# Hybrid diffusion trunk on one core: order of the first DeltaNet head's work and of the first loads

## The chip, the cores and the metric

The kernel runs on one core of a Trainium2 chip. The metric is the device time in microseconds (us) of one execution; of several executions the median. Before the change it is 2210.88 us (median of 3 runs, 2209.02 to 2216.32). A profiled execution of its own gives the trace.

TensorE (PE) does the matrix products, VectorE (DVE) and ScalarE (ACT) the elementwise work, GpSimd (POOL) a part of it, SyncE (SP) issues nearly all loads.

## The reference

A trunk of four layers works on 128 context tokens and 256 latent tokens, 1024 features wide. Layers 0 and 3 mix tokens with a gated DeltaNet, layer 1 with grouped-query attention, layer 2 with latent attention. After each mixer comes a mixture of 16 experts. Shift, scale and gate of every sub-layer come from the conditioning vectors ("ada", the modulation).

```
for l in range(DEPTH):
    m = split(silu(cond) @ w_ada[l] + b_ada[l], 6)
    h = x * (1 + m[1]) + m[0]
    o = mixer(h)                                     # gdn, gqa, mla, gdn
    x = layer_norm(ALPHA * x + (1 + m[2]) * o)
    f = moe(x * (1 + m[4]) + m[3])
    x = layer_norm(ALPHA * x + (1 + m[5]) * f)

def gdn(h):                                          # 8 heads, 128 wide
    q, k, v = silu(short_conv(h @ w_qkv))            # 5 taps
    z, a, b = h @ w_z, h @ w_a, h @ w_b
    g, beta = -exp(a_log) * softplus(a + dt_bias), sigmoid(b)
    # per chunk of 64 tokens, both directions: a unit triangular system,
    # then a scan over the chunks with a 128 x 128 state
    o = delta_rule(l2norm(q), l2norm(k), v, g, beta)
    return (rms_norm(o) * silu(z)) @ w_out
```

All is float32. The mixture takes the best group of experts and the two best in it, for each token.

## The kernel before

Tokens are columns: an activation is [128 partitions, 8 blocks of features, 384 tokens], in the tiles `bufx`, `bufh` and `bufo`. Each engine has its own instruction list, written out by hand, and engines meet through semaphores. The order in a list is the order of the code; no scheduler moves anything.

**Loads.** Weights go through `ring`, eight slots of 1 MB (2048 columns), in the fixed order of their use. SP issues a load when the slot's earlier unit has been used (`ring_free`), and counts up `ring_full` of the slot when it lands. At the start SP issues the parameters `par` (1434 columns: conditioning and its bias, 208 columns, come first; then norm gains, taps, router and the weights `w_ab` of a and b), the first two modulation units, the constants `con` (3076 columns: identity, masks, fold matrices), four more units, the input `bufx`, and two more units. Then come the first head's units. All of them use one queue.

**Start.** TensorE multiplies the eight modulation units (L742). DVE turns the rows and adds the bias (L2195, L2197). ACT and DVE modulate x into `bufh` (L1687, L2214). Then TensorE's `gdn` begins: the a/b rows (L851, reads `w_ab`), two steps of the first head's projection (L834), a fold of the a/b rows with a constant matrix (L857), the rest of the projection, and the chunk sums (L865). Before the fold ACT copies the rows to `lnt` (L1675).

**Heads.** A head's work on TensorE has four projections m = 0 to 3 (k, q, v, z), eight contraction steps each (`head_proj`, L834; a step shows as two passes in the trace), row sums (`decay_rows`, L906), Gram products (`gram`, L935), turned keys and values (`k_tokens` L945, `v_tokens` L956), an inversion by small 32 x 32 products (`invert`, L974 and others) and a scan over chunks (`scan`). The projections of head n = h + 1 are cut into pieces and put between the steps of head h's `invert` and `scan`, so that TensorE has work while ACT and DVE take a product. Projection m of head 0 goes to PSUM bank 5 if m is odd, everything else to bank 6. Raw results m = 0 to 2 are copied by ACT (semaphore `raw_in`, three per head), z by `head_z` on ACT (L1731, semaphore `z_in`, one per head). In the scan, `qe` (L1116) starts to write bank 5.

In `invert` of head h, TensorE waits for DVE's turned tile (`inv_x`, L2420), does product 1 (L974), then the first two steps of head h + 1's projection, its first row sums and the value tokens:

```
pe.wait_ge(inv_x, hh * X_STEPS + X_AT["ndt"])
product(hh, 1)
if more:
    head_proj(l, n, 0, 0, 2)
    decay_rows(l, n, 0)
v_tokens(l, h)
```

The value tokens wait for DVE's decayed keys (`kd_done`, L2398) and the third silu on ACT.

**Layer norms.** After the root, DVE multiplies eight tiles (L2245, `normed`, one each). ACT modulates tiles 0 to 4 of the next `bufh` (L1680), DVE tiles 5 to 7 (L2252, two instructions a tile). GpSimd's `scale_residual` writes ALPHA times the normalised x to `bufx` (L2935, eight instructions), for the next residual. It waits first for all of `bufh` (`wait_all_h`). In layer 3 GpSimd's `gdn` follows with three memsets of scratch (L2959 to L2961; ACT waits for them by `pad_zero`). In the mixtures TensorE multiplies the router (L1545), and a chain of small DVE instructions (L2667 to L2696) picks the experts, before TensorE goes on with L1570.

Of the kernel before, what the change touches and what calls it, by code (L numbers as in the profile page):

```python
# [360 lines left out]
def trunk(nc, I, O):  # L361

    unit_at, n_units = unit_plan()
    with ExitStack() as ctx:
# [152 lines left out]

        params_in, consts_in, x_in = sems("params_in consts_in x_in")
        ring_full = [sem(f"ring_full{i}") for i in range(RING)]
# [138 lines left out]
        def _(sp):  # L658
            sp.dma_start(par[:, :], I["params"]).then_inc(params_in, 16)

# [9 lines left out]
            for n, pair in enumerate(START_PAIRS):  # L670
                for x in range(2):
                    load(I["w_ada"][2 * pair + x], 2 * n + x)
                if n == 0:
                    sp.dma_start(con[:, :], I["consts"]).then_inc(consts_in, 16)
                if n == 2:
                    sp.dma_start(bufx[:, :, :], I["x"]).then_inc(x_in, 16)
            for l, kind in enumerate(KINDS):
                u0, uo = unit_at["mix", l], unit_at["out", l]
                if kind == "gdn":
                    order = gdn_order(l)  # L680
                    for n, (what, h, k) in enumerate(order):
                        if what == "w":
                            load(I["gdn_w_in"][li_of[l] * 2 * H + 2 * h + k], u0 + n)
                        else:
                            load(I["w_ada"][2 * ADA_AT["head", l] + 4 * h + k], u0 + n)
# [43 lines left out]
        def _(pe):  # L729
# [90 lines left out]
            def head_proj(l, n, m, k0=0, k1=KT):  # L820
# [3 lines left out]
                if k0 == 0:  # L824
                    landed(pe, u)
                    if m == 0:
                        pe.wait_ge(z_in, nn)
                    elif n:
                        pe.wait_ge(raw_in, nn * 3 + m)
                    elif m >= 2:  # L830
                        pe.wait_ge(raw_in, nn * 3 + m - 1)
# [13 lines left out]
            def gdn(l):  # L845
# [7 lines left out]
                last.then_inc(ab_mm, 1)  # L853
                head_proj(l, 0, 0, 0, 2)
                pe.wait_ge(ab_act, 2 * li + 1)
                for t in range(TT):
# [149 lines left out]
            def invert(l, h):  # L1006
# [4 lines left out]
                if h:  # L1011
                    pe.wait_ge(s_done, hh * 10)
                pe.wait_ge(inv_x, hh * X_STEPS + X_AT["ndt"])
                product(hh, 1)
                if more:
                    head_proj(l, n, 0, 0, 2)
                    decay_rows(l, n, 0)
# [72 lines left out]
            def scan(l, h):  # L1090
# [21 lines left out]
                def qe(r):  # L1112

                    for d in range(2):
                        s = SCAN[r, d]
# [540 lines left out]
            for n in range(4):  # L1656
                for x in range(2):
                    ada_unit(n, 2 * n + x, x, START_BANKS[n % 2])
            pe.wait_ge(consts_in, 16)
            for l, kind in enumerate(KINDS):  # L1660
# [9 lines left out]
        def _(act):  # L1670
# [502 lines left out]
            first_modulated(0, 4)  # L2173
            act.wait_ge(consts_in, 16)
            act.wait_ge(mod_ready, 4)
            first_modulated(4, H_ACT)
            for l, kind in enumerate(KINDS):
                {"gdn": gdn, "gqa": gqa, "mla": mla}[kind](l)
# [6 lines left out]
        def _(dve):  # L2185
# [717 lines left out]
            for n in range(4):  # L2903
                ada_add(START_PAIRS[n], 2 * n + 1, n, START_BANKS[n % 2])
            dve.wait_ge(consts_in, 16)
            for l, kind in enumerate(KINDS):
                if l == 0:
                    dve.wait_ge(x_in, 16)
                    dve.wait_ge(mod_ready, 4)
                    first_modulated()  # L2910
                else:
                    dve.wait_ge(mod_ready, (l + 1) * (ADA_UNITS // 2))
# [7 lines left out]
        def _(pool):  # L2920
# [3 lines left out]
            def scale_residual(n):  # L2924

                if n == 0:
# [4 lines left out]
                    return  # L2931
                wait_all_h(pool, n)
                for k in range(KT):
# [116 lines left out]

            pool.wait_ge(params_in, 16)
            for part, name in enumerate(("ln_g", "ln_b")):
# [93 lines left out]
```

## Time and profile before

| | us |
|---|---|
| median of 3 runs | 2210.88 |
| the profiled execution, its own time | 2213.71 |
| its span, first to last instruction | 2211.9 |
| PE busy | 2038.2 |
| DVE busy | 1339.1 |
| ACT busy | 1034.5 |
| POOL busy | 244.0 |

In the first of 40 slices of the span the queue moved 378 GB/s. Times in all views are from the start of the span, so they compare with 2211.9; what lies around the span is 1.8 us.

### The profile page before, as it was taken

The page shows a single profiled execution, that of the slowest core. Times are in us where ns is not written, and L with a number is a line of the kernel's source. Part 1 is how long each engine was busy: PE and PEld are TensorE (multiplying, and loading weights), DVE is VectorE, ACT ScalarE, POOL GpSimd, SP SyncE. Part 2 cuts the span into 40 slices and gives each one's busy share as a digit, 9 for nine tenths or more (in the row PEclk, how much of TensorE's full clock was granted, in tenths as well). Part 3 has the DMA queues.
Part 4 walks back from the last instruction along what each step waited for, and adds up shares of the span by engine and source line. Part 5 has one row for each costly group of instructions (what it writes and reads, how often), then busy time and mean ns, then how long its engine had stood idle before and what let it go on. Part 6 is the DMA issues. An engine that isn't in the chain of part 4 may idle for free.

```text
span 2211.9 us, 44967 instructions
## 1 busy us (share of the span) xinstructions
PE 2038.2 (92%) x18880; PEld 1420.3 (64%) x18881; DVE 1339.1 (61%) x2625; ACT 1034.5 (47%) x1783; POOL 244.0 (11%) x363
## 2 busy tenths in 40 slices
PE   6999999898998999899899998998899999988996
PEld 3566666557775665677666665776466666647774
DVE  2566655437896341689722325898656666437896
ACT  3344444226774341576523315765444454226773
POOL 0432222110001000100010001000322232100000
PEclk9999999998999999899999998999999999889998
DMA  9234343345895444488643443887311121025880
GB/s 378 95 131 173 121 151 148 142 153 186 284 318 203 164 173 163 145 310 297 236 151 142 152 172 131 309 303 267 117 45 64 45 69 64 26 79 181 281 299 29
DMA packets 56768, 381.22 MB, mean 172 GB/s; under 512 B 6384, under 2 KB 10480, under 8 KB 12000
## 3 DMA queue, kind: packets, MB, share of 16 engines
q1 hardware_dynamic: 51552, 373.00, 47.2%
q10 hardware_dynamic: 4608, 4.20, 0.5%
q8 instruction: 159, 2.61, 0.5%
q0 software_dynamic: 384, 0.89, 0.1%
q14 instruction: 65, 0.53, 0.1%
HBM read 373.96 MB, written 4.10 MB: 171 GB/s over the span
## 4 chain that ended last, share of the span: by engine, by line
PE 77%; DVE 13%; ACT 5%; issue 3%; DMA 1%; SPq 0%; ACTq 0%; DVEq 0%
PE ps L834 15%; PE ps L1495 6%; PE ps L1499 5%; PE ps L1498 5%; DVE e_wlo L2806 5%; PE ps L786 4%; PE ps L762 4%; PE ps L742 3%; PE ps L974 3%; PE ps L1282 3%; DVE bufx L2824 2%; PE ps L797 2%; ACT e_whi L1675 2%; PE ps L1451 2%; PE ps L1383 2%
## 5 line engine op out<-in xcount | busy, mean ns | idle before, releaser
L2806 DVE TENSOR_TENSOR e_wlo<-ring,e_whi 128x1024 fp32r<-128x1024 f32 x384 | 456.0, 1220 | 94.6 <-ACT e_whi L1675 79.2
L1675 ACT ACTIVATE e_whi<-ring 128x1024 fp32r<-128x1024 f32 x384 | 402.9, 1060 | 120.4 <-PE ps L1499 117.2
L834 PE MATMUL ps<-bufh,ring 128*128 128x384 f32 x1024 | 394.7, 507 | 6.9 <-ACT bufo L1731 4.7
L834 PEld LDWEIGHTS ps<-bufh,ring 128*128 128x128 f32 x1024 | 177.3, 192 | 98.3 <-issue 23.3
L1495 PE MATMUL ps<-e_whi,e_hs 128*128 128x512 f32 x512 | 210.7, 412 | 28.3 <-DVE e_wlo L2806 24.8
L1675 ACT ACTIVATE scratch<-ps 128x384 f32<-128x384 f32 (+6 forms) x311 | 109.1, 368 | 220.5 <-PE ps L834 52.4
L1499 PE MATMUL ps<-e_whi,e_hs 128*128 128x512 f32 x512 | 200.8, 392 | 0.0
L1498 PE MATMUL ps<-e_wlo,e_hs 128*128 128x512 f32 x512 | 199.9, 390 | 0.0
L2935 POOL TENSOR_SCALAR bufx<-bufo,x_gb 128x384 f32<-128x384 f32 x56 | 36.2, 661 | 1104.3 <-DVE bufh L2252 1104.3
L1495 PEld LDWEIGHTS ps<-e_whi,e_hs 128*128 128x128 f32 x512 | 96.0, 188 | 69.2 <-ACT e_whi L1675 41.8
L2338 DVE SCALAR_TENSOR_TENSOR scratch<-scratch,par 128x386 f32<-128x386 f32 x192 | 128.4, 669 | 4.8
L742 PE MATMUL ps<-ring,silc 128*32 128x128 f32 x3072 | 105.8, 292 | 20.1 <-DMA ring<-in_w_ada 20.1
L1675 ACT ACTIVATE scratch<-ps,scratch 128x128 f32<-128x128 f32 x96 | 31.8, 365 | 194.6 <-PE ps L1129 192.9
L1495 PE MATMUL ps<-e_whi,e_hidT 128*128 128x512 f32 x256 | 103.2, 403 | 13.3 <-issue 9.2
L1499 PEld LDWEIGHTS ps<-e_whi,e_hs 128*128 128x128 f32 x512 | 96.0, 188 | 21.9
L742 PEld LDWEIGHTS ps<-ring,silc 128*32 128x32 f32 x3072 | 87.8, 117 | 33.8 <-DMA ring<-in_w_ada 15.6
L1498 PEld LDWEIGHTS ps<-e_wlo,e_hs 128*128 128x128 f32 x512 | 96.4, 188 | 16.6
L1675 ACT ACTIVATE lnt<-ps 128x384 f32<-128x384 f32 x26 | 12.7, 490 | 195.5 <-PE ps L797 178.6
L1498 PE MATMUL ps<-e_wlo,e_hidT 128*128 128x512 f32 x256 | 102.2, 399 | 0.0
L1499 PE MATMUL ps<-e_whi,e_hidT 128*128 128x512 f32 x256 | 101.7, 397 | 0.0
L974 PEld LDWEIGHTS ps<-scratch 32*32 32x32 f32 x6144 | 64.8, 107 | 54.7 <-issue 37.2
L2224 DVE SCALAR_TENSOR_TENSOR bufh<-ps,mod,bufx 128x128 f32<-128x128 f32 x64 | 23.4, 412 | 118.9 <-PE ps L762 77.3
(312 smaller groups left out, 3525.1 us busy)
## 6 DMA issues: line engine op xcount, KB each, us to landing
ring<-in_moe SPq DMA_DIRECT2D x192, 1024.0 KB, 4.9
ring<-in_w_ada SPq DMA_DIRECT2D x96, 1024.0 KB, 6.8
ring<-in_gdn_w_in SPq DMA_DIRECT2D x32, 1024.0 KB, 6.6
ring<-in_gdn_w_out SPq DMA_DIRECT2D x8, 1024.0 KB, 4.8
ring<-in_gqa_w_in SPq DMA_DIRECT2D x6, 1024.0 KB, 4.8
ring<-in_gqa_w_out SPq DMA_DIRECT2D x4, 1024.0 KB, 6.7
ring<-in_mla_w_out SPq DMA_DIRECT2D x4, 1024.0 KB, 7.8
ring<-in_mla_w_in SPq DMA_DIRECT2D x3, 1024.0 KB, 4.9
```

The source lines that it names most:

```text
L742: last = mm(ps[32 * g:32 * g + 32, bank, 0:P], silc[:, kt, :], w[:, k, g, :], start=(kt == 0), stop=(kt == KT - 1))
L762: last = mm(ps[:, banks[t % len(banks)], 0:T], w[:, t % 2, kt, :], rhs[:, kt, :], start=(kt == 0), stop=(kt == KT - 1))
L786: last = mm(ps[:, banks[t % len(banks)], 0:T], w[:, t % 2, kt, :], bufo[:, kt, :], start=(kt == 0), stop=(kt == KT - 1))
L834: last = mm(ps[:, head_bank(n, m), 0:T], w[:, m % 2, kt, :], bufh[:, kt, :], start=(kt == 0), stop=(kt == KT - 1))
L974: last = mm(ps[quarter(g), bank, at:at + 32], g_inv[a][quarter(g), d, t, :], g_inv[b][quarter(g), d, t, :], start=True, stop=True)
L1282: last = mm(ps[:, bank, 0:T], w[:, pos % 2, kt, :], bufh[:, kt, :], start=(kt == 0), stop=(kt == KT - 1))
L1495: first = mm(out, parts[0], whi, start=start, stop=False)
L1498: mm(out, parts[0], wlo, start=False, stop=False)
L1499: return mm(out, parts[1], whi, start=False, stop=stop)
L1675: return op(out, in_, ACT.Copy, **kw)
L2338: done = stt(acc, g_cin[:, m, tap:tap + CONVW], taps[:, tap:tap + 1], acc, ALU.mult, ALU.add)
L2806: return tt_(e_wlo[:, b, :], w, e_whi[:, b, :].bitcast(F32), ALU.subtract)
```

## The change

- SP loads the parameters in two parts: the first 208 columns at the start (`params_in`), the other 1226 behind the eighth modulation unit (`rest_in`). x goes behind the fourth unit, consts behind the first head's first unit.
- The waits for consts move behind the first modulation on ACT and DVE, and behind the a/b rows on TensorE. GpSimd waits for the second part of the parameters before its first instruction.
- In `invert` of head 0, in both DeltaNet layers, the two steps of head 1's projection stand ahead of the wait for the turned tile. They wait for head 0's three raw copies, and not for its z copy. The scan's `qe` waits for z in head 0.
- GpSimd's `scale_residual` no longer waits for all of `bufh`, except for the first one.

```diff
-            sp.dma_start(par[:, :], I["params"]).then_inc(params_in, 16)
+            first_params = PARAMS["ln_g"][0]
+            sp.dma_start(par[:, 0:first_params], I["params"][:, 0:first_params]).then_inc(params_in, 16)
...
-                if n == 0:
-                    sp.dma_start(con[:, :], I["consts"]).then_inc(consts_in, 16)
-                if n == 2:
+                if n == 1:
                     sp.dma_start(bufx[:, :, :], I["x"]).then_inc(x_in, 16)
+            sp.dma_start(par[:, first_params:PARAM_COLS], I["params"][:, first_params:PARAM_COLS]).then_inc(rest_in, 16)
...
                             load(I["gdn_w_in"][li_of[l] * 2 * H + 2 * h + k], u0 + n)
+                            if l == 0 and n == 0:
+                                sp.dma_start(con[:, :], I["consts"]).then_inc(consts_in, 16)
... TensorE, head_proj
-                    if m == 0:
+                    if m == 0 and n == 1:
+                        pe.wait_ge(raw_in, nn * 3)
+                    elif m == 0:
                         pe.wait_ge(z_in, nn)
... TensorE, gdn
                 head_proj(l, 0, 0, 0, 2)
+                pe.wait_ge(consts_in, 16)
                 pe.wait_ge(ab_act, 2 * li + 1)
... TensorE, invert
+                if h == 0:
+                    head_proj(l, n, 0, 0, 2)
                 pe.wait_ge(inv_x, hh * X_STEPS + X_AT["ndt"])
                 product(hh, 1)
                 if more:
-                    head_proj(l, n, 0, 0, 2)
+                    if h:
+                        head_proj(l, n, 0, 0, 2)
                     decay_rows(l, n, 0)
... TensorE, scan, qe
+                    if r == 0 and h == 0:
+                        pe.wait_ge(z_in, hh + 1)
... TensorE, before the layers
-            pe.wait_ge(consts_in, 16)
+            pe.wait_ge(rest_in, 16)
... ACT
             first_modulated(0, 4)
-            act.wait_ge(consts_in, 16)
             act.wait_ge(mod_ready, 4)
             first_modulated(4, H_ACT)
+            act.wait_ge(rest_in, 16)
+            act.wait_ge(consts_in, 16)
... DVE
-            dve.wait_ge(consts_in, 16)
...
                     first_modulated()
+                    dve.wait_ge(rest_in, 16)
+                    dve.wait_ge(consts_in, 16)
... GpSimd, scale_residual, n > 0
-                wait_all_h(pool, n)
... GpSimd, before the layers
-            pool.wait_ge(params_in, 16)
+            pool.wait_ge(rest_in, 16)
```

On SP, the loads of the start before the change (the last number is columns):

```order
L659 DMA par<-in_params 128x1434
L664 DMA ring<-in_w_ada 128x2048 x2
L674 DMA con<-in_consts 128x3076
L664 DMA ring<-in_w_ada 128x2048 x4
L676 DMA bufx<-in_x 128x3072
L664 DMA ring<-in_w_ada 128x2048 x2
L664 DMA ring<-in_gdn_w_in 128x2048 x3
```

and after it:

```order
L660 DMA par<-in_params 128x208
L665 DMA ring<-in_w_ada 128x2048 x4
L675 DMA bufx<-in_x 128x3072
L665 DMA ring<-in_w_ada 128x2048 x4
L676 DMA par<-in_params 128x1226
L665 DMA ring<-in_gdn_w_in 128x2048
L685 DMA con<-in_consts 128x3076
L665 DMA ring<-in_gdn_w_in 128x2048 x2
```

The constants, and most of the parameters, moved from ahead of the last modulation units to behind them.

On TensorE, the end of head 0's projections and the start of its inversion, before the change (L945 turned keys, L974 small products, L906 row sums, L956 value tokens):

```order
L945 MATMUL ps<-con,scratch 128x128 x2
L834 MATMUL ps<-bufh,ring 128x384 x2
L974 MATMUL ps<-scratch 32x32 [waits inv_x]
L974 MATMUL ps<-scratch 32x32 x23
L834 MATMUL ps<-bufh,ring 128x384 [waits z_in,ring_full2]
L834 MATMUL ps<-bufh,ring 128x384
L906 MATMUL ps<-con,scratch 128x128 [waits s_done]
L906 MATMUL ps<-con,scratch 128x128 x2
L956 MATMUL ps<-con,scratch 64x128 [waits silu_done,kd_done]
```

and after it, under its own line numbers (L950 keys, L838 projection, L979 small products, L911 row sums, L961 value tokens):

```order
L950 MATMUL ps<-con,scratch 128x128 x2
L838 MATMUL ps<-bufh,ring 128x384 x2
L838 MATMUL ps<-bufh,ring 128x384 [waits raw_in,ring_full2]
L838 MATMUL ps<-bufh,ring 128x384
L979 MATMUL ps<-scratch 32x32 [waits inv_x]
L979 MATMUL ps<-scratch 32x32 x23
L911 MATMUL ps<-con,scratch 128x128 [waits s_done]
L911 MATMUL ps<-con,scratch 128x128 x2
L961 MATMUL ps<-con,scratch 64x128 [waits silu_done,kd_done]
```

The two projection steps moved from behind the first small product to ahead of it, and wait for `raw_in` where they waited for `z_in`.

## Rows read from the trace of the kernel before

**Rows 1.** Chain of waits, 0 to 75 us: start us, us, what

```profile
5.91 27.66 DMA ring<-in_w_ada
...
40.66 3.97 PE ps L834 x12
```

**Rows 2.** Timeline, 30 to 40 us: start us, us, engine line op out<-in xcount [idle before]

```profile
31.13 1.94 PE L742 MATMUL ps<-ring,silc 128*32 128x128 f32 x32 [4.24 <-DMA ring<-in_w_ada]
...
38.62 0.49 ACT L1675 ACTIVATE lnt<-ps 128x384 f32<-128x384 f32 x1 [1.81 <-PE ps L851]
```

**Rows 3.** Timeline, layer 0, 64 to 77 us, head 0's inversion

```profile
64.36 1.46 PE L834 MATMUL ps<-bufh,ring 128*128 128x384 f32 x4
...
66.70 9.72 POOL L2929 TENSOR_SCALAR bufx<-bufx 128x384 f32<-128x384 f32 x8
...
67.49 0.62 PE L974 MATMUL ps<-scratch 32*32 32x32 f32 x48 [1.68 <-DVE scratch L2420]
...
69.40 1.02 DVE L2398 TENSOR_TENSOR scratch<-ps,scratch 128x384 f32<-128x384 f32 x2
...
70.54 2.90 PE L834 MATMUL ps<-bufh,ring 128*128 128x384 f32 x4 [2.43 <-ACT bufo L1731]
...
75.87 1.05 PE L974 MATMUL ps<-scratch 32*32 32x32 f32 x96
```

**Rows 4.** Timeline, layer 3, 1600 to 1606 us, head 0's inversion

```profile
1600.19 1.02 DVE L2398 TENSOR_TENSOR scratch<-ps,scratch 128x384 f32<-128x384 f32 x2
...
1605.12 0.88 PE L956 MATMUL ps<-con,scratch 128*64 128x128 f32 x12
...
1605.92 1.05 PE L974 MATMUL ps<-scratch 32*32 32x32 f32 x96
```

**Rows 5.** Stretches: length, busy of each engine (instructions), granted clock, DMA share, GB/s

```profile
core 0: us, PE busy (x) PEld busy (x) DVE busy (x) ACT busy (x) POOL busy (x), PEclk, DMA share, GB/s
70.00:74.00 4.00, 3.46 (x8) 2.28 (x9) 0.80 (x2) 0.62 (x3) 4.00 (x4) 0.50 0.01 2
495.30:497.86 2.56, 0.40 (x4) 0.16 (x2) 2.41 (x7) 1.20 (x3) 2.56 (x5) 1.00 0.04 13
1575.00:1580.00 5.00, 5.00 (x16) 3.79 (x17) 3.49 (x8) 3.16 (x7) 0.00 (x0) 0.50 0.00 0
```

**Rows 6.** Timeline, layer 3, 1565 to 1592 us, entry of the DeltaNet

```profile
1565.06 5.16 POOL L2935 TENSOR_SCALAR bufx<-bufo,x_gb 128x384 f32<-128x384 f32 x8 [212.34 <-DVE bufh L2252]
...
1567.10 0.75 PE L857 MATMUL ps<-con,lnt 128*128 128x32 f32 x6
...
1570.20 3.06 DVE L2275 TENSOR_SCALAR scratch<-scratch 128x48 f32<-128x48 f32 x1
...
1573.58 1.55 PE L865 MATMUL ps<-scratch,con 128*128 128x24 f32 x8 [1.78 <-DVE scratch L2279]
...
1591.58 0.88 PE L935 MATMUL ps<-scratch 128*64 128x128 f32 x12
```

**Rows 7.** Timeline, layer 0, 39 to 61 us, the same three operations

```profile
39.91 0.75 PE L857 MATMUL ps<-con,lnt 128*128 128x32 f32 x6
...
44.45 0.97 PE L865 MATMUL ps<-scratch,con 128*128 128x24 f32 x8
...
60.54 0.88 PE L935 MATMUL ps<-scratch 128*64 128x128 f32 x12
```

**Rows 8.** Timeline, layer 0, 489 to 499 us, layer norm and router

```profile
489.72 1.01 DVE L2245 TENSOR_TENSOR bufo<-bufh,ps 128x384 f32<-128x384 f32 x2
...
490.65 1.82 DVE L2252 TENSOR_SCALAR bufh<-bufo,h_gb 128x128 f32<-128x128 f32 x6
...
495.83 0.17 DVE L2674 TENSOR_TENSOR lnt<-lnt 128x24 f32<-128x24 f32 x1
...
498.96 0.39 PE L1570 MATMUL ps<-e_rs,con 128*128 128x12 f32 x1 [3.26 <-DVE e_rs L2696]
```

**Rows 9.** Timeline of DVE, L2335 with GpSimd idle and with it busy

```profile
45.24 0.42 DVE L2335 TENSOR_SCALAR scratch<-scratch,par 128x386 f32<-128x386 f32 x1 [1.35 <-ACT scratch L1675]
...
65.47 0.81 DVE L2335 TENSOR_SCALAR scratch<-scratch,par 128x386 f32<-128x386 f32 x1
```

More of the change, by code:

```diff
@@ L515, in trunk @@
         e_cnt = sb("e_cnt", [P, NG])
-        params_in, consts_in, x_in = sems("params_in consts_in x_in")
+        params_in, rest_in, consts_in, x_in = sems("params_in rest_in consts_in x_in")
         ring_full = [sem(f"ring_full{i}") for i in range(RING)]
```

## The prediction, on record before the changed kernel ran

> **What bounds the kernel now.** I read the chain of waits of the first 75 us, then the timeline of the same stretch, then the same places in layer 3, then the layer norms. The start is bound by the loads: the chain goes from 5.91 us through one DMA of 27.66 us, the last of the eight modulation units; it lands at 5.91 + 27.66 = 33.57, and from there the projections of TensorE (L834) are in the chain [rows 1]. The reader is to see that nothing on an engine sets the first 33 us, only bytes on one queue: units arrive 33.57 - 31.13 = 2.45 us apart [rows 1, 2]. After that TensorE is almost always busy, and what can be won are its holes. Two alike are around the first head of each DeltaNet layer. In layer 0 TensorE ends a projection at 64.36 + 1.46 = 65.82, waits 1.68 us for DVE, does one product (0.62), waits 2.43 us for the z copy on ACT, and then runs four passes of the next projection in 2.90 us where the same four took 1.46 just before, because the granted clock is 0.50, its lower level of 1.2 GHz [rows 3, 5]. Layer 3 has the same picture [rows 4].
>
> **The head's projection.** The first two contraction steps of head 1's projection (four passes of L834) go ahead of the wait for the turned tile, and wait for the three raw copies only. Their bank was last read by the third raw copy, long done at 65.8; their weights came before the holes. So they fill 65.8 to 67.3 and the product still starts at 67.49. What is late next: six passes of row sums (L906), done near 69.0, then the value tokens (L956), which wait for DVE's L2398, ending at 69.40 + 1.02 = 70.42 [rows 3]. Twelve passes of L956 take 0.88 at the full clock [rows 4]. The two products of L974 that started at 75.87 then start at 70.42 + 0.06 + 0.88 = 71.36: 4.5 us earlier. In layer 3: 1600.19 + 1.02 + 0.06 + 0.88 = 1602.15 instead of 1605.92, 3.8 us earlier [rows 4]. What follows is the same cadence of products and ACT and DVE steps, moved as a whole. The new wait for z in front of the scan's first L1116 costs nothing: z is copied just before 70.54, the products at 75.87 come after that, and the scan after the products [rows 3]; behind the wait stand only passes of the same head. What hides the row sums, the wait for L2398, leaves 1.5 us of TensorE idle; see the clock below.
>
> **The loads.** By the last modulation unit 3076 columns of consts and 1226 of 1434 columns of parameters are no longer ahead. At 2.45 us for 2048 columns that is 3.68 + 1.47 = 5.15 us: it lands at 28.42. The rest of the parameters lands at 29.89, the head's first unit at 32.34, the consts at 36.02. TensorE needs the parameters at about 29.8 for L851 and the head unit at 33.5, so neither costs more than 0.1. But ACT now takes the consts before its copy of the a/b rows. That copy started at 38.62, 5.05 after the last unit [rows 1, 2]; by the unit alone it would start at 33.47, by the consts at 36.07. So the fold (L857) starts at 36.07 + 0.49 (the copy) + about 0.36 (hand-over and weights, an estimate) = 36.92 instead of 39.91 [rows 2, 7]: 3.0 us, not 5.15. Bounds: 0, if the queue gives the consts no earlier than that they are needed now, and 5.15. I take 3.0. GpSimd starts its pads only when the rest of the parameters is there, at 30, and its three memsets took the length of the 3.06 us row at 1570.20 [rows 6]; they end near 34, before ACT first writes into them (about 39). The queue carries the same bytes in all, so the head's second unit lands as before, at 36.02 + 2.45 = 38.5; TensorE comes to it only after passes that end at 40.66 + 3.97 = 44.6 [rows 1].
>
> **The wait taken from GpSimd's residual scaling.** Eight instructions (L2935, 5.16 us in one run) now start behind the first normalised tile and not behind the last modulated one, in seven layer norms. It gives back in two places. First the entry of layer 3. Now the run ends at 1570.2, the memsets follow, and DVE's L2275, 48 columns, takes 3.06 us beside them [rows 6]; TensorE idles 1.78 and the clock is 0.50 from 1575 to 1580 [rows 5, 6]. From the fold to the chunk sums (L857 to L865) layer 0 needs 44.45 - 39.91 = 4.54, layer 3 1573.58 - 1567.10 = 6.48; from there to the Gram products (L935) layer 0 needs 16.09 and layer 3 18.00 [rows 6, 7]. The excess is 1.94 + 1.91 = 3.85, all of which goes if run and memsets are past. Second, the router of every mixture: seven DVE instructions took 2.41 us beside the run where one free of it takes 0.17 [rows 5, 8]. 2.41 - 7 x 0.17 = 1.2, with their overlap about 1.3, and TensorE waits 3.26 us for them [rows 8].
>
> It takes in a third place. The run now lies beside DVE's normalising (L2245) and its six modulating instructions (L2252, 1.82 us), whose end TensorE waits for at once in the router and in layer 3 [rows 8]. L2245 has one input in SBUF; L2398, of the same kind and size, took 1.02 for two with GpSimd busy beside it [rows 3], and two of L2245 with it idle take 1.01 [rows 8]: no cost. L2252 is a tensor_scalar; that kind (L2335) took 0.42 alone and 0.81 beside GpSimd [rows 9], 0.39 more. With three pairs, each waiting once, that is 3 x 0.39 = 1.2, less the slack of the sixth; I take 1.0 per norm. Bounds: 0, and 2.0, if L2252 waits until the whole run is over (it starts 0.55 after L2245 and lasts 5.16; L2252 starts 3.73 after it). In the attention layers the first projection is long enough to hide it. So a mixture gains 1.3 - 1.0 = 0.3, four give 1.2 (bounds -2.8 and 5.2), and layer 3 gains 3.85 - 1.0 - 0.3 = 2.5, the 0.3 for the memsets that now lie beside the first DVE step of the a/b rows (bounds 1.5 and 3.85).
>
> The Trainium skill (SBUF — State Buffer, Practical consequences) says that a DVE instruction with at most one SBUF input and outside the two-port modes does not contend with GpSimd, and that tensor_scalar in such a mode does, the second to issue waiting for the whole of the other's instruction. The trace agrees on both kinds, by the 1.02 against 1.01 and the 0.81 against 0.42 above. It speaks against this part of the change; by it each of the three GpSimd instructions left in the run would hold L2252 for its full length, and the sum would be the first rival's.
>
> **The sum.** 3.0 (start) + 4.5 + 3.8 (heads) + 2.5 (layer 3) + 1.2 (mixtures) = 15.0. From it goes an allowance for the clock. At three places TensorE idles 1.5 to 1.7 us: before the fold at the start, and before the value tokens in both heads. It fell to 1.2 GHz after a hole of 1.78 and after 1.68 and 2.43 with a product between [rows 3, 5, 6]; four passes then cost 2.90 - 1.46 = 1.4 more. One chance in two at each of three places: 2.1. Net 12.9. The profiled execution took 2213.71 (2211.88 span), so it would be 2200.8; the median of the runs before is 2210.88, 2.8 lower, so I forecast 2198.
>
> **Rivals.**
> First, DVE waits out the run in every norm that counts: 2.0 instead of 1.0 at five places, 5 us less, 2203. For it: L2275 was held for all three memsets [rows 6]. Against: in the router DVE got in between instructions of the run, seven within 2.41 us [rows 5]. Chance 0.15.
>
> Second, the heads give nothing: what follows head 0 is paced by the steps of ACT and DVE, or by a clock that falls in the new hole, and the products don't start earlier. 8.3 less in the sum, 2206. For it: an idle of 1.5 remains. Against: none of L2398 and ACT's copies waits for the moved passes. Chance 0.12.
>
> Third, the mixtures gain more: a router hole of 3.26 that becomes 2 or less keeps the clock up for the gathers behind it, some 2 us each, 8 more: 2190. Against: a second hole follows in each router, which may drop it all the same. Chance 0.12.
>
> Fourth, on the other side: the normalising L2245 itself waits for GpSimd. Paced by the run's 5.16 / 8 = 0.65, each of 8 instructions in 7 norms would take up to 0.65 more, 36 us in all: 2198 + 36 = 2234. It decides from 12.9 / 56 = 0.23 us per instruction. Against it stands the 1.02 of L2398. Chance 0.04.
>
> The forecast keeps 0.57. A difference under 0.3%, 6.6 us, can't be told from none. Forecast and third rival are faster, the first rival (7.9 gained) mostly, the second (4.9) is mostly the same: faster 0.80, same 0.14, slower 0.06. The range goes from the third rival with some of its gain left out, 2188, to the second with the upper bounds of DVE's wait, 2207.
>
> **What would show it.** The last modulation unit lands near 28.4, and ACT's first copy waits for the consts, at 36. In both DeltaNet layers the four passes lie ahead of the first product, there is no wait for the z copy, and the passes take 1.5, not 2.9. In layer 3 L2275 takes 0.2 and TensorE has no hole before L865. L2935 starts under L2245; L2252 takes 2.2 to 3.8 in place of 1.82; the seven router instructions take 1.2. Wrong would be a last unit that still lands after 31, L2245 above 0.6 each, or a clock that falls at places where it did not.

## The result and the profile after

| | before | after |
|---|---|---|
| median, us (runs) | 2210.1 (4, 2209.02 to 2216.32) | 2187.2 (4, 2182.55 to 2189.56) |
| the profiled execution, us | 2213.71 | 2186.74 |
| its span, us | 2211.9 | 2184.9 |
| its mean granted clock | 0.966 | 0.973 |

The ratio is 0.9888, with a 95% interval of 0.9863 to 0.9913. By the medians the kernel became 22.9 us faster, where 12.9 was forecast (2198, range 2188 to 2207). The direction was right and the size was wrong: 2187.2 lies just below the range.

I went through the trace of after in the order of the prediction's terms, each time with the same TensorE instruction in both traces: how much earlier does it start now? Lines of the kernel have moved: L834 is L838 now, L857 L862, L865 L870, L906 L911, L935 L940, L956 L961, L974 L979, L1545 L1555, L1570 L1580, L2245 L2256, L2252 L2263, L2275 L2286, L2398 L2409, L2935 L2946.

**The start.** First the timeline of after, 26 to 38 us, of TensorE, DVE and ACT in turn (start us, us, engine line op out<-in xcount [idle before]).

```profile
28.82 1.08 PE L744 MATMUL ps<-ring,silc 128*32 128x128 f32 x32 [0.82 <-DMA ring<-in_w_ada]
30.36 0.85 PE L855 MATMUL ps<-bufh,par 128*32 128x384 f32 x8 [0.46 <-DMA par<-in_params]
...
37.45 0.82 PE L862 MATMUL ps<-con,lnt 128*128 128x32 f32 x6 [1.21 <-ACT lnt L1685]
```

```profile
30.59 3.27 DVE L2225 TENSOR_SCALAR bufh<-bufx,mod 128x128 f32<-128x128 f32 x6
```

```profile
36.82 0.49 ACT L1685 ACTIVATE lnt<-ps 128x384 f32<-128x384 f32 x1 [5.32 <-DMA con<-in_consts]
```

The last modulation unit came near 28.8, and the fold waits for the consts, as forecast. They landed some 0.7 us later than I had worked out (ACT's copy, released by them, starts at 36.82), and the fold starts at 37.45 instead of 39.91 [rows 2, 7]: 2.5 us earlier for a forecast 3.0.

**The head of layer 0.** The timeline of TensorE in after, 61 to 72 us, answers to [rows 3].

```profile
61.98 2.75 PE L838 MATMUL ps<-bufh,ring 128*128 128x384 f32 x8
65.10 0.62 PE L979 MATMUL ps<-scratch 32*32 32x32 f32 x48 [0.38 <-DVE scratch L2431]
65.65 0.93 PE L911 MATMUL ps<-con,scratch 128*128 128x128 f32 x6
68.09 0.88 PE L961 MATMUL ps<-con,scratch 128*64 128x128 f32 x12 [1.50 <-DVE scratch L2409]
68.90 1.05 PE L979 MATMUL ps<-scratch 32*32 32x32 f32 x96
69.87 1.56 PE L838 MATMUL ps<-bufh,ring 128*128 128x384 f32 x4
```

The picture is the forecast one: the wait of 1.68 is 0.38, the wait of 2.43 for the z copy is gone, and one of 1.50 for L2409 is left. The four moved passes are the last of the eight in the first row, which take 2.75 together: about 1.4 for four, and not 2.90. (The four of 69.87 are the next two steps, which were there before.) The product pair starts at 68.90 instead of 75.87. Of these 6.97 us 2.4 came from the start, so the head gave 4.6, forecast 4.5.

**The entry and the head of layer 3.** The timeline of TensorE in after, 1551 to 1592 us.

```profile
1553.81 0.75 PE L862 MATMUL ps<-con,lnt 128*128 128x32 f32 x6
...
1558.35 0.97 PE L870 MATMUL ps<-scratch,con 128*128 128x24 f32 x8
...
1574.42 0.88 PE L940 MATMUL ps<-scratch 128*64 128x128 f32 x12
...
1584.24 1.54 PE L961 MATMUL ps<-con,scratch 128*64 128x128 f32 x12 [1.38 <-DVE scratch L2409]
1585.71 1.50 PE L979 MATMUL ps<-scratch 32*32 32x32 f32 x96
```

Two rows of DVE, from its timeline of 1544 to 1560 us, are its modulating instructions and the one that had been held:

```profile
1548.89 2.70 DVE L2263 TENSOR_SCALAR bufh<-bufo,h_gb 128x128 f32<-128x128 f32 x6
...
1556.56 0.19 DVE L2286 TENSOR_SCALAR scratch<-scratch 128x48 f32<-128x48 f32 x1
```

The hole of 1.78 before the chunk sums is gone, and DVE's L2286 takes 0.19 where L2275 had taken 3.06. Fold to chunk sums is 1558.35 - 1553.81 = 4.54, the same as in layer 0; on to the Gram products it is 16.07. So 1.94 + 1.93 = 3.9 came in, as worked out, and 0.9 was paid ahead of it, where L2263 takes 2.70 and L2252 took 1.82. In this head the clock did fall in the hole that the edit leaves: twelve passes of L961 take 1.54, not 0.88. The pair of products starts at 1585.71 instead of 1605.92, 20.2 earlier, and 17.2 of it was there at the Gram products: 3.0 for the head, forecast 3.8.

**The mixtures.** The timeline of DVE and then of TensorE in after, in the norm and the router of layer 0, answers to [rows 8].

```profile
486.15 2.71 DVE L2263 TENSOR_SCALAR bufh<-bufo,h_gb 128x128 f32<-128x128 f32 x6
...
491.69 0.18 DVE L2684 TENSOR_TENSOR lnt<-lnt 128x24 f32<-128x24 f32 x1
```

```profile
493.83 0.39 PE L1580 MATMUL ps<-e_rs,con 128*128 128x12 f32 x2 [1.73 <-DVE e_rs L2707]
```

L2263 takes 2.71 where L2252 took 1.82: the 0.9 that it pays for running beside GpSimd, forecast 1.0. The router's wait is 1.73 instead of 3.26: 1.5 gained, forecast 1.3. The difference, 0.6, is what the instructions themselves give; 0.3 was forecast. But a mixture gave more than that. From the norm to 20 us behind the router the four gained 2.0, 3.4, 2.0 and 1.2 us in this trace. (Counted from the first L2245 of the norm to the first product with an expert's weights, some 21 us behind the rank products L1570; 0.5 to 0.6 of each gain is there when the rank products start, the rest comes behind them.) Three stretches show where, as busy time of the engines and the granted clock: 32 us from the norm of mixtures 0 and 1, and 22 us at the end of layer 3's mixer, first before, then after.

```profile
487.00:519.00 32.00, 23.71 (x173) 19.23 (x166) 21.93 (x70) 16.01 (x29) 5.76 (x11) 0.71 0.18 69
893.00:925.00 32.00, 23.91 (x173) 18.67 (x166) 22.00 (x70) 16.20 (x31) 5.75 (x11) 0.73 0.19 69
...
1918.00:1940.00 22.00, 20.03 (x116) 14.78 (x116) 5.50 (x19) 2.58 (x7) 1.56 (x4) 0.61 0.02 7
```

```profile
481.00:513.00 32.00, 25.20 (x182) 19.66 (x182) 21.42 (x71) 17.55 (x31) 6.07 (x11) 0.73 0.23 82
884.00:916.00 32.00, 24.83 (x187) 19.28 (x186) 22.27 (x71) 18.39 (x34) 6.06 (x11) 0.79 0.20 69
...
1900.00:1922.00 22.00, 19.81 (x136) 13.52 (x135) 9.22 (x24) 3.14 (x9) 1.56 (x4) 1.00 0.02 7
```

The columns are those of [rows 5]; the one to read is the granted clock, the third from the end: 0.71 and 0.73 before, 0.73 and 0.79 after. Behind the routers TensorE runs for less time at 1.2 GHz. At the end of layer 3's mixer the clock is 1.00 instead of 0.61, worth 6 us in this pair, at a place which the change doesn't touch.

So the terms at the instructions held, and what is left to explain, some 10 us, looks like clock. Theory A: the routers' shorter hole keeps the clock up, and GpSimd's part of the change gives far more than its instructions do. Theory B: work is moved as a whole, and the clock falls elsewhere by luck, whichever part moves it.

### The profile page after: what moved, and what is told of

Same layout as the page of the kernel before. It is cut to its first block, busy times and chain, and to the rows that moved or that the text cites. A ratio compares the mean times of both kernels' runs of the same rounds, so it can differ in the third digit from the quotient of the medians.

```text
span 2184.9 us, 44966 instructions
## 1 busy us (share of the span) xinstructions
PE 2021.1 (92%) x18880; PEld 1403.4 (64%) x18881; DVE 1338.0 (61%) x2625; ACT 1034.3 (47%) x1783; POOL 246.5 (11%) x363
## 4 chain that ended last, share of the span: by engine, by line
PE 76%; DVE 13%; ACT 5%; issue 4%; DMA 2%; ACTq 0%; SPq 0%; DVEq 0%
PE ps L838 15%; PE ps L1505 6%; DVE e_wlo L2817 5%; PE ps L1509 5%; PE ps L1508 5%; PE ps L788 4%; PE ps L764 4%; PE ps L744 3%; PE ps L979 3%; PE ps L1292 3%; DVE bufx L2835 2%; PE ps L799 2%; PE ps L1461 2%; ACT e_whi L1685 2%; PE ps L1393 2%
## 5 line engine op out<-in xcount | busy, mean ns | idle before, releaser
L838 PE MATMUL ps<-bufh,ring 128*128 128x384 f32 x1024 | 392.4, 505 | 2.0 <-ACT scratch L1685 0.7
L838 PEld LDWEIGHTS ps<-bufh,ring 128*128 128x128 f32 x1024 | 177.0, 191 | 93.9 <-issue 18.3
L1505 PE MATMUL ps<-e_whi,e_hs 128*128 128x512 f32 x512 | 210.5, 411 | 28.2 <-DVE e_wlo L2817 24.8
L2946 POOL TENSOR_SCALAR bufx<-bufo,x_gb 128x384 f32<-128x384 f32 x56 | 37.6, 685 | 1072.5 <-DVE bufo L2256 1072.5
L979 PEld LDWEIGHTS ps<-scratch 32*32 32x32 f32 x6144 | 65.5, 108 | 55.9 <-issue 40.5
```

What stands on the lines that cost most here:

```text
L838: last = mm(ps[:, head_bank(n, m), 0:T], w[:, m % 2, kt, :], bufh[:, kt, :], start=(kt == 0), stop=(kt == KT - 1))
L979: last = mm(ps[quarter(g), bank, at:at + 32], g_inv[a][quarter(g), d, t, :], g_inv[b][quarter(g), d, t, :], start=True, stop=True)
L1505: first = mm(out, parts[0], whi, start=start, stop=False)
```

## Experiments

Twelve experiments, in three groups of four; each group shared one chip and its own runs of the kernel before. Gains below are (1 - ratio) times the median of before in that group (2208.75, 2211.12 and 2210.5 us), with the interval's ends. They can be up to 3.5 us off the plain difference of the medians. By this formula the first comparison above is 24.8 (19.2 to 30.3).

### The three parts alone, and the whole once more

`only_head` has the edits in `head_proj`, `invert` and `scan`, `only_loads` those of the loads and the waits for them, and `only_pool` is this line alone:

```diff
             def scale_residual(n):
...
-                wait_all_h(pool, n)
```

> The kernel before with the head's part alone: in the first head of both DeltaNet layers the two steps of the next projection go ahead of the wait for the turned tile. Theory A (the steps of my sum are right where they stand, and what was mis-sized is the clock in the mixtures): the product pair behind head 0 starts 4.5 us earlier in layer 0 and 3.8 in layer 3, with 1 to 4 us given back behind them by the clock, so 4 to 8 us less than before; the mixtures stand as before, within 1 us each. Theory B (the 22.9 us come from this part, by work that is moved as a whole to other phases of the clock): 12 us or more less. The second rival of the prediction (the heads give nothing): within 2 us of before.

> The kernel before with the loads' part alone: parameters in two parts, x and consts moved, and the waits for them. Theory A: the fold of the a/b rows starts 2.5 us earlier, all that follows moves with it, and the time is 1 to 3 us less; the mixtures are as before. Theory B (the clock falls at other places only because everything is moved in time, whichever part moves it): the mixtures and the end of layer 3's mixer change by 2 us or more each here too, in either direction, and the time is 5 us or more off from before.

> The kernel before with GpSimd's part alone: the residual scaling no longer waits for the whole modulated tile. By the prediction's terms: 2.5 for the entry of layer 3 and 0.3 for each of four mixtures, 3.7 us less. Theory A (a router chain that is 1.5 us shorter keeps the granted clock up through the gathers behind it): 2 to 4 us less in each mixture, 3 at the entry of layer 3, so 10 to 17 us less in all, the half-clock stretch behind the router 10 to 14 us long in place of 17, and the first hole of each router 1.7 us in place of 3.3. Theory B (moved phases): 3 to 5 us less. The fourth rival of the prediction, or anything that GpSimd beside the normalising costs: over 0, slower than before.

> The changed kernel once more, beside the parts of it. Theory A: about 23 us less than before, and the three parts alone add up to this within 4 us. Theory B: the parts don't add up, since each moves the clock's falls in its own way; their sum is 8 us or more off.

| kernel | median us (runs) | ratio, 95% | gain us |
|---|---|---|---|
| only_head | 2199.56 (12) | 0.9949, 0.9930 to 0.9968 | 11.3 (7.1 to 15.5) |
| only_loads | 2209.20 (12) | 0.9994, 0.9974 to 1.0014 | 1.3 (-3.1 to 5.7) |
| only_pool | 2197.44 (12) | 0.9941, 0.9919 to 0.9963 | 13.0 (8.2 to 17.9) |
| after_again | 2181.89 (5) | 0.9873, 0.9842 to 0.9904 | 28.1 (21.2 to 34.9) |

The parts add up to 11.3 + 1.3 + 13.0 = 25.6 against 28.1. That is within the 4 us of theory A, but with intervals of 4 to 7 us on each of the four figures the sum can't exclude theory B's 8. What speaks against B is `only_pool`: 3 to 5 expected by it, 13.0 measured, and 8.2 is the lower end.

GpSimd's part gives 13.0 where its terms came to 3.7; that is the part that was mis-sized. The head's 11.3 is over the 4 to 8 that theory A expected and near the 12 of theory B; its interval holds 8.3, the two terms of the prediction, and 12 as well. In its trace the two heads give 4.6 and 3.8. The loads' 3.0 is inside their interval too, and so is 0: in the trace the fold starts 3.0 us earlier, the ratio gives no more than 1.3, and the two medians differ by 0.4 us the other way.

Theory B's expectation for the loads came half true: in that one trace the end of layer 3's mixer gained 6 us also, and the four routers, whose hole is still 3.26 (2.75 in the fourth), lost 0.8 to 1.4 each. `pool_l3`, below, leaves the routers alone too, and in its trace one loses 1.0 and one 2.6. So a single trace moves by as much as 2.6 us at a router with nothing changed there. Which places the clock picks does differ from one execution to the next, as in the two profiles of the changed kernel: 119 to 123 us, first in one, then in the other.

```profile
119.00:123.00 4.00, 3.30 (x65) 2.33 (x66) 0.35 (x1) 2.17 (x4) 0.00 (x0) 0.60 0.02 8
```

```profile
119.00:123.00 4.00, 4.00 (x93) 2.89 (x82) 1.80 (x4) 2.66 (x6) 0.69 (x2) 1.00 0.02 4
```

The Trainium skill (TensorE: Matmul & The Clock Gate, Part 1) says, of the start of a kernel, that how many products run at the lower clock varies from run to run. These two rows show the same of a fall in its midst: same kernel, same stretch, 0.60 and 1.00. It means that a single pair of profiles can't price the clock; a dozen runs of each can, to within 4 or 5 us.

### GpSimd's part, cut in two, and the clock alone

`pool_moe` takes the wait away ahead of the four mixtures only, `pool_l3` ahead of layer 3 only (`if n != 6:` in front of it, and `if n % 2 == 0:` for the first). `before_fill` is the kernel before with this:

```diff
+                for _ in range(4):
+                    mm(ps[:, 5, 0:T], ones, bufh[:, 0, :], start=True, stop=True)
                 pe.wait_ge(oh_ready, l + 1)
```

> The kernel before, and GpSimd's scaling freed of its wait only in the four norms ahead of the mixtures. By the prediction's terms 0.3 a mixture: 1.2 us less, which can't be told from none. Theory A (the router's chain is 1.5 shorter, DVE pays 0.9, and the shorter hole leaves less time at the lower clock behind it): 2 us less a mixture, so 8 us less, 5 to 12; the half-clock stretch behind each router begins later or is shorter than 17 us. The first hole of each router is 1.73 instead of 3.26 under both.

> The kernel before, and GpSimd's scaling freed of its wait only in the norm ahead of layer 3. By the prediction 2.5 us less, by the traces so far 3.0: the stretch from the fold of the a/b rows to the Gram products 3.9 shorter, the stretch before it 0.9 longer. Under every theory so far the mixtures stand as before. A time over 6 us less would say that moving layer 3 as a whole is worth something by itself.

> The kernel before, with nothing of the change; TensorE multiplies four times 384 columns with ones, ahead of its wait in the router (3.26 us of idling) in every mixture; nobody reads the results. The chain of DVE stays as long as before, so no term but the clock can gain. Theory A (the hole before the gathers costs the clock, and with it about 2 us in every mixture): 4 to 10 us less than before, and the 17 us at half clock behind the router shrink. Theory B (the clock would fall all the same, by the second hole or by itself): within 2 us of before, or slower by what the products hold TensorE up.

| kernel | median us (runs) | ratio, 95% | gain us |
|---|---|---|---|
| pool_moe | 2200.65 (12) | 0.9952, 0.9933 to 0.9970 | 10.6 (6.6 to 14.8) |
| pool_l3 | 2207.67 (12) | 0.9992, 0.9971 to 1.0013 | 1.8 (-2.9 to 6.4) |
| before_fill | 2194.64 (12) | 0.9941, 0.9920 to 0.9962 | 13.0 (8.4 to 17.7) |

The mixtures are the place: 10.6 us where the prediction had 1.2. In the trace of `pool_moe` the four gain 8.0 together, 2.7 of it ahead of the rank products and 5.3 behind them. Layer 3's entry gives 1.8 by the ratio, with 0 in the interval, and 3.0 in its trace, forecast 2.5.

`before_fill` settles the mechanism. It makes nothing earlier; it only gives TensorE something to do in the hole, and it gains 13.0 us, over the 4 to 10 that theory A expected, where theory B had at most 2. The timeline of TensorE at its first router: the chain of DVE ends where it did, relative to the norm, but the idle time before the rank products is 0.68 and not 3.26 [rows 8].

```profile
500.22 2.75 PE L1570 MATMUL ps<-bufh,con 128*128 128x384 f32 x8
503.65 0.39 PE L1572 MATMUL ps<-e_rs,con 128*128 128x12 f32 x2 [0.68 <-DVE e_rs L2698]
```

The stretches of 32 us of routers 1 and 2, of before, of `pool_moe` and of `before_fill`:

```profile
893.00:925.00 32.00, 23.91 (x173) 18.67 (x166) 22.00 (x70) 16.20 (x31) 5.75 (x11) 0.73 0.19 69
1341.00:1373.00 32.00, 23.69 (x176) 18.47 (x176) 21.98 (x70) 16.27 (x31) 5.75 (x11) 0.73 0.19 71
```

```profile
892.00:924.00 32.00, 24.83 (x187) 19.25 (x188) 21.57 (x71) 18.81 (x33) 6.07 (x11) 0.79 0.21 74
1338.00:1370.00 32.00, 24.76 (x182) 18.46 (x180) 21.34 (x70) 17.44 (x32) 6.06 (x11) 0.79 0.20 74
```

```profile
893.00:925.00 32.00, 25.34 (x185) 18.48 (x178) 22.84 (x71) 18.14 (x32) 5.75 (x11) 0.89 0.19 69
1338.00:1370.00 32.00, 24.96 (x190) 18.09 (x182) 23.03 (x71) 18.37 (x33) 5.75 (x11) 0.89 0.19 69
```

In these rows a hole of 3.26 goes with 0.73, one of 1.73 with 0.79, one of 0.68 with 0.89; other traces scatter around that, see the last section. In the trace of `before_fill` the four mixtures gain 3.5, 3.0, 2.9 and 1.0 us, all behind the hole: from the norm to the rank products it takes 12.0 us (12.2 in the fourth), as before. So by this trace a wait in the router cost its own length and 1 to 3.5 us after it.

### Later and filled

`pool_late` is the changed kernel with one line more, so that the scaling lies beside the gathers:

```diff
+                if n % 2:
+                    pool.wait_ge(flags_ready, n // 2 + 1)
                 for k in range(KT):
                     pool.wait_ge(normed, KT * (n - 1) + k + 1)
```

`router_fill` is the changed kernel with two filling products ahead of the router's wait, as in `before_fill`. `late_fill` has both edits. `late_fill2` has in addition

```diff
+                for _ in range(4):
+                    mm(ps[:, 5, 0:T], ones, bufh[:, 0, :], start=True, stop=True)
                 pe.wait_ge(flags_ready, l + 1)
                 crowded = pe.value_load(flags[0:1, 0, 2:3], min_val=0, max_val=1)
```

and `late_all` in addition to that, on GpSimd,

```diff
                 G.memset(g_cin, 0.0).then_inc(pad_zero, 1)
+                if l:
+                    scale_residual(2 * l)
...
-                if l + 1 < DEPTH:
+                if l + 1 < DEPTH and KINDS[l + 1] != "gdn":
                     scale_residual(2 * l + 2)
```

> The changed kernel, with one difference: ahead of the mixtures GpSimd's eight scaling instructions wait until the router has its flags, so they lie beside the gathers, neither beside DVE's modulating nor beside the router's small instructions. The 0.9 us that DVE's L2252 of the kernel before loses beside them comes back in each of four mixtures, and the router's hole stays at 1.73: 3.6 us less than the changed kernel, about 2180 where that takes 2183. Against it: if DVE's work beside the gathers is held by GpSimd and TensorE waits for it, the gain is gone, and the time is that of the changed kernel or up to 3 us over it.

> The changed kernel, and two products of 384 columns with ones in TensorE's wait of the router (1.73 us) in every mixture; nobody reads their results. What the hole costs by the clock is then left over from the change: 1 to 2 us a mixture where the half-clock stretch began at this hole. Theory A: 3 to 7 us less than the changed kernel, about 2179 where that takes 2184, and no half-clock stretch over 7 us behind a router. Theory B: the same time.

> The same filling, in the kernel in which GpSimd's scaling ahead of the mixtures waits for the router's flags. That one was 0 to 4 us slower than the changed kernel, where 3.6 less was expected; its trace has the 0.9 us of DVE's wait back in mixtures 0 and 1, and stretches of 17 and 20 us at half clock behind the routers of mixtures 2 and 3. If only the clock took the gain, this one takes 3 to 4 us less than the filled kernel without the delay, about 2176. If GpSimd beside the gathers costs something, it is no faster than that one.

> As the last, and four more products of 384 columns ahead of TensorE's second hole in each router (5.3 us, while the flags are read and branched on). If TensorE's instructions run on while it waits, they lie in the hole, and the clock stays up through the gathers: the last stretches of 3 to 7 us at half clock behind the routers go, up to 2 us less a mixture, about 2170. Against it: if the wait for the flags can't be taken before the products have run, each mixture pays 1 to 2.5 us for them, and the time is 2176 to 2184.

> As the last, and ahead of layer 3 GpSimd does its three memsets first and the eight scaling instructions behind them. DVE's modulating of that norm then runs with GpSimd idle: 0.9 us back. Against it: the scaling now lies beside DVE's steps on the a and b rows, 48 columns each; if they are held as L2275 of the kernel before was, up to 3 us are lost.

| kernel | median us (runs) | ratio, 95% |
|---|---|---|
| pool_late | 2187.16 (6) | 0.9892, 0.9867 to 0.9917 |
| router_fill | 2184.33 (5) | 0.9883, 0.9861 to 0.9905 |
| late_fill | 2180.43 (5) | 0.9870, 0.9847 to 0.9892 |
| late_fill2 | 2174.91 (5) | 0.9843, 0.9823 to 0.9862 |
| late_all | 2182.24 (5) | 0.9877, 0.9855 to 0.9900 |

`pool_late` shows nothing of its 3.6 us, though its interval, 18.4 to 29.4 us of gain, is too wide to exclude them. Its step is right, in DVE's timeline of the first norm:

```profile
486.06 1.82 DVE L2263 TENSOR_SCALAR bufh<-bufo,h_gb 128x128 f32<-128x128 f32 x6
```

The 1.82 of before is back, with 0.9 of the time. But the wait of 1.73 is still there, and in this trace, of the slowest of its six runs, the clock went down early behind routers 2 and 3. The four mixtures gain 7.6 against before, less than the 8.6 of the changed kernel's trace:

```profile
1323.00:1355.00 32.00, 24.72 (x179) 20.60 (x179) 21.00 (x71) 17.46 (x32) 5.78 (x11) 0.68 0.23 83
1958.00:1990.00 32.00, 23.61 (x107) 18.37 (x108) 20.74 (x68) 16.21 (x29) 5.22 (x9) 0.58 0.01 3
```

`router_fill` doesn't show its 3 to 7 us either: 2184.33 against 2180.39 to 2189.56 in the nine runs of the changed kernel, none of them in this group. The clock of its first three routers did rise to 0.89, but two things in its trace, again that of its slowest run (2192.35), took that back. At the end of layer 3's mixer it has the stretch at 0.61 that before has. And behind router 3 TensorE's second hole, in which it reads the flags and branches, is 8.1 us long, where it is 5.3 in the changed kernel. The waits of TensorE over 20 us there, in `router_fill` and then in the changed kernel (engine line, waited for: us in total, times, longest):

```profile
PE ps L1461 <- issue: 8.1, 1, 8.1
```

```profile
PE ps L1461 <- issue: 5.3, 1, 5.3
```

`late_fill` has the long one too (7.84), and the earlier three routers of both have not. The profile shows no wait for data behind it, and I can't say what makes it longer. `late_fill2` has the same two products and four more, and does not have it: there the gathers of router 3 start 2.24 us behind the last product.

`late_fill` takes 2180.43, 3.9 less than `router_fill`, which is the 3 to 4 less that was expected if only the clock had taken the gain of `pool_late`. With five runs each, from 2176.75 to 2185.72 and from 2179.41 to 2192.35, this difference is not shown.

`late_fill2` did what it was expected to do, except that it stopped at 2174.91 and not at 2170; that is 5.5 below `late_fill` on the same chip. The products ahead of the flags run while TensorE's sequencer waits, reads and branches: the gathers behind router 0 start at 497.65, 3.04 after the products, and the clock stays up.

```profile
491.11 0.91 PE L1597 MATMUL ps<-con,e_sid 128*128 128x128 f32 x6
491.87 2.75 PE L1602 MATMUL ps<-bufh,con 128*128 128x384 f32 x8
497.65 1.66 PE L1461 MATMUL ps<-e_pick,e_hi 128*128 128x256 f32 x12 [3.04 <-issue]
```

```profile
474.00:506.00 32.00, 25.70 (x205) 17.46 (x202) 21.18 (x71) 19.54 (x35) 5.81 (x11) 1.00 0.29 108
876.00:908.00 32.00, 26.53 (x205) 18.60 (x206) 23.14 (x72) 20.00 (x34) 5.81 (x11) 1.00 0.21 79
1320.00:1352.00 32.00, 26.87 (x201) 19.22 (x202) 22.57 (x72) 19.29 (x33) 5.81 (x11) 0.95 0.22 77
1946.00:1978.00 32.00, 26.01 (x134) 18.37 (x135) 21.46 (x69) 18.85 (x33) 5.26 (x9) 0.79 0.01 3
```

From 0.71 to 0.73 in before the clock of the first three routers went to 1.00, 1.00 and 0.95. The mean clock of its five runs is 0.984, that of before's eleven 0.965. It is the fastest kernel here: 35.6 us below before by the medians, 34.7 (30.5 to 39.1) by the ratio. Its slowest run (2178.16) is below the fastest of the changed kernel's nine (2180.39), though none of those ran in this group.

`late_all` was meant to give 0.9 more or to lose up to 3; it is 7.3 us slower than `late_fill2`. At the entry of layer 3 its trace has the 0.9. What it lost lies elsewhere in that trace: 4 us in layer 0, which has three falls of the clock from 250 to 410 us where `late_fill2` has one, and 6 at the end of layer 3's mixer. One profile doesn't show whether that goes with the kernel or with the run, and the cause of the 7.3 stays open.

## Why the prediction was wrong

**Right, step by step.** The loads: 3.0 forecast, 2.5 and 3.0 in two traces of the changed kernel. In the first the wait for the consts is next, as named; in the second TensorE comes to the fold without idling. (The 0.36 us for hand-over and weights came from no row; here it took 37.45 - 36.82 - 0.49 = 0.14.) The head of layer 0: 4.5 forecast, 4.6. The head of layer 3: 3.8 forecast, 3.0 here and 3.8 in `only_head`, the difference being the clock's fall in the hole that the allowance had named. The entry of layer 3: 2.5 forecast, 3.9 - 0.9 = 3.0; the 0.3 set down for the memsets did not come, DVE's first step on the a/b rows took 0.21 as before. DVE's wait beside GpSimd: 1.0 forecast, 0.9. The second rival (the heads give nothing) fell with `only_head`, 11.3 us. The fourth fell too: L2256 takes 0.55 an instruction, as L2245 did. So did the first: 2.71 and not 3.8 for L2263. The Trainium skill (SBUF — State Buffer, Practical consequences) has the one that comes second blocked while the other's instruction holds the shared ports. The six instructions paid 0.9 together, 0.15 each, where a GpSimd instruction takes 0.65 to 0.78. So here it was on average far less than one whole such instruction, which fits a wait for what is left of one; that each waited so is not shown.

**Wrong: the term of the mixtures.** "So a mixture gains 1.3 - 1.0 = 0.3, four give 1.2" counted the instructions only. Measured by `pool_moe` it is 10.6 (6.6 to 14.8), 9.4 over the term, and the forecast missed by 22.9 - 12.9 = 10.0. At the instructions a mixture gives 1.5 - 0.9 = 0.6, so 2.4 of the 10.6. The rest, 8 by the ratio and 5.3 in the trace of `pool_moe`, is the clock behind the router, which `before_fill` shows to be worth 13.0 (8.4 to 17.7) when the hole is nearly closed and nothing else is done. This was my third rival, which gave 2190 with "8 more" at a chance of 0.12. What I set against it, that a second hole follows in each router and may drop the clock all the same, is half right: the clock does fall all the same, but later and for less time. In before it falls at the end of the first hole of the first three routers, within 1.1 us of the rank products, and stays down for 17 us. In the first trace of the changed kernel it falls 1.4 to 6.1 us behind them, in two of the four routers only in the second hole, for 7 to 14 us; in `before_fill` 5.3 to 8.2 us behind them, for 3 to 7 us.

**Wrong: the sign of the clock's allowance.** I took the clock as a loss only: three new holes at 1.4 us each, one chance in two, -2.1. I didn't ask the same of the holes that the change takes away, although the row of before with 0.50 behind a hole of 1.78 [rows 5, 6] was the reason for the allowance. Of the three new holes one cost its clock in this trace (layer 3), two did not; in the second trace of the changed kernel none did. The prediction also took falls at places where there were none before as a sign of being wrong: the stretch from 119 to 123 us is one.

**What stays open.** The profiled pair differs by 27.0 us, the medians by 22.9: the stretch at 0.61 at the end of layer 3's mixer is in the traces of before, `only_head`, `router_fill` and `late_all`, at 1.00 in both of the changed kernel, and gone or shorter in all others, `only_loads` and `before_fill` among them. So 6 of the 19.7 us between the profiles of before and `before_fill` are this stretch too, and 10.4 the mixtures. Whether it goes with a kernel or with an execution, one profile of each can't tell.

## What to carry to other kernels

When TensorE bounds a kernel and its clock falls behind short holes, price a hole as its length and what the work after it pays at 1.2 GHz, and do that for the holes that a change closes as well as for those that it opens. Look at the granted clock of the stretch behind each wait that a change shortens, before summing instructions. If a hole can't be closed, products that nobody reads may be worth as much as an edit of the chain before it: here 13.0 us (8.4 to 17.7) against 10.6 (6.6 to 14.8). And price the clock by many runs, never by two profiles.

## What the runs showed of the hardware

The same hole went with different clocks in different executions. Over 32 us from the norm it was 0.71 to 0.73 in before, with a hole of 3.26 us (2.75 at the fourth router); with the same hole it was 0.68 in `only_loads` and 0.63 to 0.79 in `only_head`. It was 0.73 to 0.79 in the first profile of the changed kernel, with 1.73, and 0.68 to 0.84 in the second; but with the same 1.73 `pool_late` had 0.58 and 0.68 in two of its four. It was 0.84 to 0.89 in `before_fill`, with 0.68 and less. That a shorter hole pays shows over a dozen runs, and can fail in a single execution.

TensorE's clock also fell behind shorter idling: in layer 3 it was at 1.2 GHz behind the hole of 1.38 us in one trace of the changed kernel, and at 2.4 GHz behind one of 1.39 us in the other.

Four products of 384 columns (2.75 us with the way they are spaced) placed ahead of a wait, a read of flags and a branch cost nothing at the first router. From the products of L1597 to the gathers it is 497.65 - 491.11 = 6.54 us in `late_fill2`, and 497.23 - 490.69 = 6.54 in `late_fill`, which has no such four.

TensorE's wait "issue" ahead of the gathers can grow by 2.8 us, from 5.3 to 8.1, in one of four places with the same code, when two products a mixture were added to the program; with four more it did not. The runs don't show why.
